# Key tiles of a cross attention moved into three stage boundaries of a fused two-block decoder kernel

## The reference

```python
def reference(x, c, positions, ..., mem_2, ...):
    x = first_block(x, c, positions, ...)
    return second_block(x, mem_2, ...)
```

```python
def cross_attention(h, mem, wq, wkv, wo):
    q = (h @ wq).reshape(B, S, X_HEADS, X_HEAD_DIM)
    k, v = jnp.split(mem @ wkv, 2, axis=-1)
    k = k.reshape(B, M, X_HEADS, X_HEAD_DIM)
    v = v.reshape(B, M, X_HEADS, X_HEAD_DIM)
    s = jnp.einsum("bshd,bmhd->bhsm", q, k).astype(jnp.float32) / math.sqrt(X_HEAD_DIM)
    p = jax.nn.softmax(s, axis=-1).astype(v.dtype)
    o = jnp.einsum("bhsm,bmhd->bshd", p, v).reshape(B, S, X_HEADS * X_HEAD_DIM)
    return o @ wo
```

## Time and profile before

| what | us |
|---|---|
| runs | 1763.84, 1765.99, 1769.26 |
| median | 1765.99 |
| span of the profiled execution, first to last instruction | 1764.7 |
| mean granted TensorE clock | 0.993 of full |
| boundary ahead of feed-forward three | 597.86 to 606.36 |
| boundary ahead of the latent attention | 802.7 to 810.78 |
| boundary ahead of the hybrid mixer | 1140.2 to 1151.51 |
| cross attention, end of the mixer's output product to first value product | 1452.30 to 1479.74 |

### The profile page before, as it was taken

One profiled execution on the slowest core, in us unless ns is written; L12 is line 12 of the kernel. 1 busy time (PEld: TensorE's weight loads), 2 busy tenths in 40 slices (PEclk: granted clock), 3 DMA queues, 4 the chain that ended last, 5 costly groups with the idle time before them and its releaser, 6 DMA issues.

```text
span 1764.7 us, 31956 instructions
## 1 busy us (share of the span) xinstructions
PE 1669.9 (95%) x11230; PEld 1500.6 (85%) x11230; DVE 1290.2 (73%) x2161; ACT 933.4 (53%) x1664; POOL 86.6 (5%) x151
## 2 busy tenths in 40 slices
PE   6899999999999999999999999999988899999998
PEld 5899989888999889998777888898976789988886
DVE  6888888768888888876566666679888565456665
ACT  1544457644444544445575555555467845555553
POOL 2000010300000100000000000000000000000000
PEclk9999999999999999999999999999999999999999
DMA  8888866757888888865433766444633155446561
GB/s 348 311 295 297 306 173 204 156 203 249 300 292 307 236 293 302 294 184 175 131 108 70 240 191 185 148 148 151 186 97 91 49 191 168 143 136 198 191 184 65
DMA packets 123657, 352.76 MB, mean 200 GB/s; under 512 B 9851, under 2 KB 52875, under 8 KB 114225
## 3 DMA queue, kind: packets, MB, share of 16 engines
q1 hardware_dynamic: 108128, 262.18, 46.4%
q10 hardware_dynamic: 12432, 78.65, 13.8%
q0 software_dynamic: 3008, 10.74, 1.9%
HBM read 347.31 MB, written 4.22 MB: 199 GB/s over the span
## 4 chain that ended last, share of the span: by engine, by line
PE 55%; DVE 20%; issue 11%; ACT 8%; DMA 4%; ACTq 1%; POOL 1%; DVEq 0%; POOLq 0%; SPq 0%
PE ps L829 36%; PE ps L1062 8%; PE ps L1063 4%; DVE w_lo L195 4%; DVE arena L358 4%; DVE arena L2680 2%; ACT w_hi L1116 2%; ACT w_hi L189 2%; DVE w_lo L1127 1%; DMA gate_scratch<-gcol 1%; DMA resid<-in_x 1%; DVE resid L1322 1%; DVE act_s L1196 1%; DMA grow<-gate_scratch 1%; ACTq L332 1%
## 5 line engine op out<-in xcount | busy, mean ns | idle before, releaser
L829 PE MATMUL ps<-t_both,w_hi 128*128 128x256 f32 x3952 | 725.9, 285 | 10.1 <-DVE t_both L758 5.7
L829 PEld LDWEIGHTS ps<-t_both,w_hi 128*128 128x128 f32 x3952 | 615.0, 191 | 23.5 <-issue 10.6
L829 PE MATMUL ps<-t_both,w_lo 128*128 128x256 f32 x1976 | 558.5, 283 | 1.3 <-issue 1.3
L195 DVE TENSOR_TENSOR w_lo<-raw,w_hi 128x1024 fp32r<-128x1024 f32 x240 | 288.6, 1222 | 122.6 <-ACT w_hi L189 122.4
L829 PEld LDWEIGHTS ps<-t_both,w_lo 128*128 128x128 f32 x1976 | 376.6, 191 | 0.2
L1127 DVE TENSOR_TENSOR w_lo<-raw,w_hi 128x1024 fp32r<-128x1024 f32 x258 | 313.6, 1221 | 83.0 <-ACT w_hi L1116 82.9
L1116 ACT ACTIVATE w_hi<-raw 128x1024 fp32r<-128x1024 f32 x258 | 268.8, 1053 | 120.2 <-PE ps L829 79.2
L189 ACT ACTIVATE w_hi<-raw 128x1024 fp32r<-128x1024 f32 x240 | 248.2, 1053 | 143.1 <-PE ps L829 99.6
L1062 PE MATMUL ps<-t_both,w_hi 128*128 128x512 f32 x640 | 226.7, 398 | 0.0
L829 PE MATMUL ps<-w_hi,g_hi 128*128 128x512 f32 x440 | 176.8, 402 | 14.4 <-DVE g_lo L1199 11.9
L1063 PE MATMUL ps<-t_both,w_lo 128*128 128x256 f32 x640 | 179.7, 281 | 0.0
(11 more groups left out here) (378 smaller groups left out, 1662.4 us busy)
## 6 DMA issues: line engine op xcount, KB each, us to landing
raw<-in_stream SPq DMA_DIRECT2D x498, 512.0 KB, 4.5
arena<-in_mod_w ACTq DMA_DIRECT2D x72, 1024.0 KB, 7.2
grow<-gate_scratch POOLq DMA_DIRECT2D x6, 512.0 KB, 7.7
u_scratch<-u_keep ACTq DMA_DIRECT2D x1, 3072.0 KB, 36.8
arena<-u_scratch POOLq DMA_DIRECT2D x8, 256.0 KB, 3.3
small<-in_small POOLq DMA_DIRECT2D x1, 1368.0 KB, 11.2
resid<-in_x POOLq DMA_DIRECT2D x1, 1024.0 KB, 18.9
arena<-in_mem POOLq DMA_DIRECT2D x1, 1024.0 KB, 5.4
```

Source lines behind the costliest of these rows:

```text
L195: VE.tensor_tensor(w_lo[:, s, :], raw[:, s, :], w_hi[:, s, :].bitcast(F32), ALU.subtract).then_inc(lo_done, 1)
L829: last = TE.matmul(out, lhs, rhs, start=start and i == 0, stop=stop and i == 2)
```

## The change

The memory is loaded behind the norm of feed-forward two, turned by TensorE in bodies 1 and 2 of that feed-forward (which therefore leave the loop), kept in high parts (ScalarE, which also copies the bank for GpSimd) and low parts (GpSimd) in the arena, stored to DRAM during feed-forward three, loaded back ahead of feed-forward four, and loaded back again in two pieces in the hybrid mixer. Key tiles 0 and 1 are made ahead of the turn of the tokens in the boundary ahead of feed-forward three, 2 and 3 in that ahead of the latent attention, 4 and 5 in that ahead of the hybrid mixer, and 6 there behind the turn. Tile 7 stays in the cross attention. Each boundary's keys are copied from PSUM by ScalarE behind the turn and stored to DRAM; seven are loaded at the end of the hybrid mixer. The stream's order (`ring_order`, `piece_of`) puts the key blocks where they are used. The fillers of the three boundaries go, the banks of the turn are given out anew (the last tiles share a bank with earlier ones and wait until these are emptied), and one block is split within `squares` at the first of the boundaries. The owed low part is paid within `squares` at all three. `x_split(4, ...)` in the cross attention moves from behind the value product to beside its fifth block, and `mod_swap` gets another place.

```diff
@@ squares / turn
+            if splits is not None:
+                pay_lo()
...
+            for _i in range(splits or 0):
+                owed[0] -= 1
+                next_split()
             return diag_at
...
+                diag_at = squares(src, src_ready, late_mod, splits=None if keys is None else keys["splits"])
+                if keys is not None:
+                    for i, to in enumerate(keys["before"]):
+                        key_tile(to, mem_at, keys["ready"])
...
+                    if kt in shares:
+                        if shares[kt] % 2 == 0:
+                            pe.wait_ge(V.sem, emptied[shares[kt]])
+                        else:
+                            pe.wait_ge(A.sem, emptied[shares[kt]])
...
             turned["at"] = (V.n, A.n)
+            if keys is not None:
+                for to in keys["behind"]:
+                    key_tile(to, mem_at, keys["ready"])
+                keys_keep(*keys["keep"])
+                turned["at"] = (V.n, A.n)
             pay_splits()
@@ new functions
+        def mem_turn(pe, g):
+            if g == 0:
+                pe.wait_ge(mem_in, 16)
+            else:
+                pe.wait_ge(mem_kept, 2 * g)
+            for k in (2 * g, 2 * g + 1):
+                for q in range(QT):
+                    last = TE.transpose(ps[6][:, k % 2 * L + q * P:k % 2 * L + (q + 1) * P], mem_raw[:, q, k * P:(k + 1) * P], ident)
+            last.then_inc(mem_turned, 1)
+
+        def mem_hi(act, g):
+            act.wait_ge(mem_turned, g + 1)
+            if g >= 2:
+                act.wait_ge(mem_lowered, g - 1)
+            E.activation(mem_tiles[:, 4 * g:4 * g + 4:2, :], ps[6][:, :].rearrange("p (a b) -> p a b", b=L),
+                         ACT.Copy).then_inc(mem_kept, 1)
+            E.activation(mem_copy[:, g % 2, :], ps[6][:, :], ACT.Copy).then_inc(mem_kept, 1)
+
+        def mem_lo(pool, g):
+            pool.wait_ge(mem_kept, 2 * g + 2)
+            GE.tensor_tensor(mem_tiles[:, 4 * g + 1:4 * g + 4:2, :], mem_copy[:, g % 2, :].rearrange("p (a b) -> p a b", b=L),
+                             mem_tiles[:, 4 * g:4 * g + 4:2, :].bitcast(F32), ALU.subtract).then_inc(mem_lowered, 1)
...
+        def key_tile(to, tiles, ready):
+            h = blocks["pe"]
+            blocks["pe"] += 1
+            s = h % RING
+            @block.tensor
+            def _(pe):
+                pe.wait_ge(lo_done, h + 1)
+                pe.wait_ge(ready[0], ready[1])
+                for k in range(KT):
+                    ws = slice(k * P, (k + 1) * P)
+                    last = triple(to, tiles(k, 0), tiles(k, 1), w_hi[:, s, ws], w_lo[:, s, ws], True, k == 0, k == KT - 1)
+                last.then_inc(used, 1)
+            owed[0] += 1
...
+        def keys_keep(first, n, banks, at):
+            done = blocks["pe"]
+            held = ar(at, n * L)
+            @block.scalar
+            def _(act):
+                act.wait_ge(used, done)
+                for i in range(0, n, 2):
+                    wide = min(2, n - i) * L
+                    E.activation(held[:, i * L:i * L + wide], banks[i // 2][:, 0:wide], ACT.Copy).then_inc(A.sem, A.up())
+            kept = A.n
+            @block.gpsimd
+            def _(pool):
+                pool.wait_ge(A.sem, kept)
+                pool.dma_start(key_dram[:, first * L:(first + n) * L], held).then_inc(keys_stored.sem, keys_stored.up(16))
@@ act_body of ffn
                     if mod is not None and more:
                         mod_load(act, t, mod + 1)
+                    if mems:
+                        mem_hi(act, mems[t])
@@ ffn
+                    if turn_mem:
+                        emit(1, 2, with_mod, (0, 1))
+                        emit(2, 3, with_mod, (2, 3))
+                    emit(3 if turn_mem else 1, FG - 1, with_mod)
...
                     emit(n_mod - 1, n_mod, with_mod)
+                    mem_store()
@@ the three boundaries
-        norm_x(..., late_mod=PRE + 2 * FG, late_load=True, busy=7)
+        norm_x(..., late_mod=PRE + 2 * FG, late_load=True,
+               keys=dict(before=halves(ps[6]), behind=(), ready=(mem_lowered, 4), splits=1,
+                         banks=(4, 5, 0, 1, 2, 7, 3, 0), shares={7: 2}, keep=(0, 2, (ps[6],), 15056)))
...
-        norm_x(..., early=2, busy=7)
+        norm_x(..., early=2,
+               keys=dict(before=halves(ps[6]), behind=(), ready=(mem_lowered, 4), splits=0,
+                         banks=(2, 4, 0, 1, 5, 7, 3, 0), shares={7: 2}, keep=(2, 2, (ps[6],), 15056)))
...
-        norm_x(lambda k, n: col("mix", k, n), early=2, busy=5, after_squares=keep_positions)
+        norm_x(lambda k, n: col("mix", k, n), early=2, after_squares=keep_positions,
+               keys=dict(before=halves(ps[6]), behind=halves(ps[3])[:1], ready=(mem_back, 16), splits=0,
+                         banks=(2, 4, 0, 1, 5, 7, 1, 0), shares={6: 3, 7: 2}, keep=(4, 3, (ps[6], ps[3]), 11504)))
@@ cross attention
-        turn(lambda q: memt[:, q, :], KT)
         add_residual(None)
         out_used = blocks["pe"]
+        acc_free[0], acc_free[1] = (x_ready[0, 1], 0), (x_ready[1, 1], 0)
         x_diag = squares(lambda q: x[:, q, :], dict(x_ready))
-        turned["at"] = (V.n, A.n)
-        columns_product(8, evac_q(kx))
+        pay_splits()
+        key_tile(ps[4][:, 0:L], mem_again, (mem_back, 48))
...
-        rows_product(KT, D, put_off=True)
+        rows_product(KT, D, put_off=True, chained=True, operand=mem_again)
```

More of the change, by code:

```diff
@@ L12 @@
 from contextlib import ExitStack
+import itertools
 import math
@@ L76, with ring_order, piece_of @@
 UP_ORDER = (9, 10, 0, 1, 2, 3, 4, 5, 11, 12, 6, 7, 8)
+THIRD_FFN, LATENT_IN, HYBRID_IN, MEM_KEYS = 169, 235, 331, 400
+AHEAD = {THIRD_FFN: (0, 1), LATENT_IN: (2, 3), HYBRID_IN: (4, 5, 6)}
+def ring_order():
+    early = [MEM_KEYS + t for tiles in AHEAD.values() for t in tiles]
+    order = []
+    for b in range(N_BLOCKS):
+        order += [MEM_KEYS + t for t in AHEAD.get(b, ())]
+        if b not in early:
+            order.append(b)
+    return order
+def piece_of(b):
+    for base in (BY_TILE, BY_TILE + 8, BY_TILE + 16, Z_BY_TILE, LATENT):
+        if base <= b < base + 8:
+            return base, ((b - base) + 6) % 8 if base == LATENT else b - base
+    if AB_OUT <= b < AB_OUT + 12:
+        return None, b + 8 if b < AB_OUT + 4 else b - 4
+    if UP <= b < UP + 13:
+        return None, UP + UP_ORDER[b - UP]
+    return None, b
 def build(nc, a):
@@ L285, in _ @@
+            rounds = n_stream // RING
+            for back, run in itertools.groupby(range(1, rounds), back_of):
+                run = list(run)
+                if back is not None and len(run) > 1:
+                    in_order(run[0], run[-1] + 1, back)
+                else:
+                    for h in range(run[0] * RING, (run[-1] + 1) * RING):
+                        one(h)
+            for h in range(rounds * RING, n_stream):
                 one(h)
@@ L778, in turn @@
                 for k in (kt, kt + 1):
-                    transpose_tile(k, (1,) if by_tokens else (0, 1))
+                    transpose_tile(k, (1,) if by_tokens and k not in shares else (0, 1))
                 empty_tile(kt)
@@ L1325, in _, with halves @@
                         x_ready[q, f] = V.n
+        def halves(bank, n=2):
+            return [bank[:, i * L:(i + 1) * L] for i in range(n)]
         def norm_x(gain, mods=None, ready=None, mods_before=0, early=4, late_mod=None, late_load=False, busy=0,
-                   after_squares=None):
+                   after_squares=None, keys=None):
             if mods is not None:
```

177 lines of the change are left out of this document (118 added, 59 removed).

## The result

Over twenty runs of each kernel the median went from 1765.78 us (1763.67 to 1769.26) to 1768.28 us (1765.22 to 1773.62). The ratio is 1.0014, with a 95% interval from 1.0008 to 1.002: 2.5 us slower (1.4 to 3.5), inside the 0.3% that counts as no change, but on the other side of zero from the forecast of 1764.2 us. The profiled execution of the changed kernel has a span of 1768.5 us; its time was 1770.6 us, 2.1 more, and 2.3 above the median.

What follows compares the result with a forecast made beforehand. TensorE, busy for 95% of the span, was taken as the bound. Terms -24.6 + 2.8 + 3.4 + 5.8 + 10.8 = -1.8 us, from the median 1765.99, gave 1764.2 us; own range 1760.5 to 1768, reaching toward rivals 1755.5 to 1770.

Steps and rivals of the forecast that it cites:

- The reload of 2 MB: Memory reload ahead of the hybrid mixer, in feed-forward four: hidden under a low DMA share, priced at nothing.
- The cross attention: Output product to value product: one key tile stays of 27.44 us, key reload hidden, value product doesn't wait; gain 24.6 us.
- Boundary one: Ahead of feed-forward three: two keys delay the turn 2.5 us, late low parts add 0.9; cost 3.4, bounds 2.5 and 4.9.
- Boundary two: Ahead of the latent attention: five owed low parts delay angles, sines and squares; cost 4.3 plus 1.5 for the clock, 5.8 us.
- the clock, 1.5 us: Behind the 3.4 us wait ahead of boundary two's token sums: TensorE's clock falls, cost 1.5 us, bounds 0 and 3.5.
- Boundary three: Ahead of the hybrid mixer: three keys, 3.4 us wait ahead of the narrow product, clock 1.5; cost 10.8, bounds 5.9 and 12.8.
- Feed-forward two: Memory's work in bodies 1 and 2: ScalarE copies 1.6 us, GpSimd beside VectorE 1.2; cost 2.8, bounds 0.5 and 4.
- GpSimd's contention: Feed-forward two: GpSimd's four low parts stretch VectorE's work by 0.3 us each, 1.2 us; 5.8 if VectorE stood still.
- The first (no waits behind the keys): Rival: VectorE catches up, blocks split in time; boundaries cost 2.5 + 2.2 + 5.9, sum -11.2, 1754.8 us; chance 0.25.
- The second: Rival: clock stays low some 7 us after each of the three boundary gaps; sum +5.7, 1771.7 us; chance 0.09.
- The third: Rival: gate row 6 us late, costing 4, 1768.2 us, chance 0.07; with VectorE stretched by 5.8, 1772.8, chance 0.04.
- the signs that were to show the prediction wrong: Narrow product right behind key 6, feed-forward two growing under 1 or over 5 us, or the value product waiting.

Runs made afterwards that it cites:

- experiment 4: Changed kernel with the 2 MB memory reload issued after the first body of feed-forward four instead of at its entrance; one execution, feed-forward four 186.33 us.
- experiment 1: Changed kernel with the memory reload issued after five bodies of feed-forward four instead of at its entrance; 1763.71 us, ratio 0.9991 to the kernel before.
- experiment 2: Kernel before with an unused 2 MB load added at the entrance of feed-forward four; 1769.72 us, ratio 1.0016 to the kernel before.
- experiment 7: Changed kernel with VectorE's angles at boundary two made behind two of the five low parts, not all five; 1763.84 us, ratio 0.9995 to before.
- experiment 3: Kernel before with an unused 1 MB load added at the entrance of feed-forward four; one execution, feed-forward four 188.04 us.
- Experiment 5: Changed kernel with boundary three's next weight block split inside the norm instead of behind the key copies; 1764.28 us, ratio 0.9984 to before.
- experiment 9: Changed kernel with the memory's four low parts in feed-forward two made by VectorE instead of GpSimd; one execution, feed-forward two 200.34 us.

## Why the prediction was wrong, step by step

**The step that failed** is the sentence "The reload of 2 MB runs under a feed-forward whose DMA share is low", and its price of nothing. It measured 4.16 us. The mean share is indeed no more than 0.64 in that stage before the change, and it was zero just ahead of the issue. But the reload was issued 0.4 us ahead of the ring's first load, at the start of the 24 us in which the DMA engines are taken for over nine tenths. ScalarE waited 8.23 us for a block instead of 2.67, VectorE's and then TensorE's work followed, and behind the 2.25 us gap the clock fell, as it did in all six profiles with the reload at this place and in none without it. Adding the load to the kernel before costs 3 us, taking it away from this place gives 4.7 (the stage is then 0.6 us shorter than before the change, which nothing here explains), and 13 us later it costs nothing; in five further profiles with the reload at the entrance the stage took 191.0 to 193.3 us. So the reload and its place are shown as the cause; what of the entrance's traffic it hinders is open (experiment 4). Without this step the forecast was good: 1764.2 us, against 1763.71 for the kernel of experiment 1.

**The cross attention**, -24.6: -24.63. The value product did not wait; no row shows a price of the key reload.

**Boundary one**, 3.4: 2.60 in the pair of profiles, 3.6 in the means. The 2.60 are made of 2.32 of delay (2.5 forecast) and 0.28 of late low parts (0.9 forecast). TensorE's gap in the first body went from 0.81 to 1.66 us, as forecast. The late low parts cost their 0.9 after all, once profiles with the same clock are compared: feed-forward three without a drop of the clock takes 195.17 us in experiment 2, whose code there is before's, and 196.18 in the changed kernel, 195.96 in experiment 7's.

**Boundary two**, 5.8: 5.25 in the pair, 5.6 in the means. Two steps were right to a tenth of a microsecond: a wait of 3.4 us, released by the squares, measured 3.34; and the clock, 1.5 us, measured 1.59. The start of the first product was delayed by 1.7, not 2.2, in the pair. Before's boundary took 8.51 us there and 8.34 and 7.43 in the kernels of experiments 2 and 3, which have its code, so that against their mean the delay is 2.1. Experiment 7 shows the chain of causes: five low parts, then angles, sines, squares.

**Boundary three**, 10.8: 9.19 + 1.53. Wait of 3.4 us ahead of the narrow product: 3.26. Experiment 5 shows that it hung on the high part behind the key copies. The three keys paid here 10.7 us, and 4.2 more for their reload, to save 8.6 in the cross attention. The gap at this boundary was 2.8 us, room for one:

```profile
1144.08 1.38 PE L425 MATMUL ps<-cst 128*128 128x128 f32 x10
1146.87 3.92 PE L697 MATMUL ps<-arena,resid 128*128 128x128 f32 x32 [1.41 <-ACT arena L578]
```

**Feed-forward two**, 2.8: 1.84. The drop of the clock at 438 is gone, as forecast, but it was not credited. That it is gone says little: in the kernels of experiments 2 and 3 the gap of 2.48 us is still there, and the clock did not fall behind it. Without the drop the stage takes 195.7 us in these two, so the memory's work costs 2.4. GpSimd's contention was put at 1.2 and is some 0.8 by the stretched rows, if body 2 is like body 1.

**The rivals.** The first (no waits behind the keys) is refuted at both places. The second had the clock low for 7 us behind each gap. Behind the narrow product's gap it was 3.4 us each time that it fell, at a price of 1.5; ahead of the token sums it was 3.4 us in three profiles and 6.8 in three, at 1.6 and 2.5; behind boundary one's gap of 1.66 us it never fell. The third had the right kind of cause, transfers, but at the wrong DMA: the store beside feed-forward three landed in 9.2 us, where 11 to 24.5 were thought of. None of the signs that were to show the prediction wrong occurred, as none of them looked at feed-forward four.

**What the single pair of profiles hides.** The rows up to feed-forward two (+1.77) and the mixer (+2.05) differ in this pair by chance, the clock's above all. At the start, eight transposes near 43 us took 1.07 us before and 1.95 in the changed kernel, where the clock was still low; over eleven kernels with the change's code the first product of feed-forward two starts between 401.03 and 404.70, and before's in three profiles between 401.33 and 403.28. In the mixer it was low for 10.2 us in the changed kernel (below). Without those two rows the stages of the pair add to -0.06 us, while the medians say +2.5: before's own profile is slow from feed-forward two to feed-forward four, 551.6 us where experiments 2 and 3, with its code there, took 549.5 and 549.4. The means over all profiles, given with the stages above, close most of that gap; they are rough, with three profiles of before's code.

## What to carry to other kernels

A low DMA share, be it the mean of a stage or the share at the moment of issue, doesn't make a transfer free: ask which transfers are issued just behind it, and when their data is needed. Here 2 MB ahead of the ring's refill cost 4 us or more, and the same 2 MB 13 us later cost nothing, although the DMA engines were then full. Work is worth moving only into a gap that is there: two keys at boundary one cost 3.6 us and save 5.8, three at boundary three cost more than they save until the wait behind them was taken out. Where an entrance has one order of instructions on each engine, adding up that order predicted the two waits within 0.2 us (3.34 and 3.26, both put at 3.4), and putting one split earlier or three low parts later took them away; the first cost nothing that the stages show, the second 1.0 us.

## What the runs showed of the hardware that was not expected

**The clock behind a gap is not the same each time.** In body 1 of feed-forward three all fourteen profiles have the same gap of 2.44 to 2.50 us; behind it the granted clock fell to 1.2 GHz in eleven and stayed at 2.4 GHz in three, the changed kernel's among them. Behind the 3.3 us ahead of the token sums it fell in six of eight. Behind 2.44 to 2.48 us in body 1 of feed-forward two, in the three profiles with before's code, it fell in one; behind 1.91 us in experiment 9's kernel it fell too. Windows of the changed kernel behind the wait of the token sums and in body 1 of feed-forward three, then of experiment 1's kernel behind the wait of the token sums (the last three numbers are the granted clock, the DMA share and GB/s):

```profile
834.00:838.00 4.00, 4.00 (x24) 4.00 (x25) 1.98 (x3) 0.67 (x1) 0.72 (x1) 0.62 0.87 246
...
648.00:652.00 4.00, 3.59 (x19) 3.10 (x20) 3.37 (x5) 2.40 (x3) 0.00 (x0) 1.00 0.84 306
```

```profile
833.50:837.50 4.00, 4.00 (x35) 4.00 (x36) 2.06 (x3) 0.75 (x1) 0.72 (x1) 1.00 0.83 250
```

The same gap of the same work thus gave both outcomes. The Trainium skill, "TensorE: Matmul & The Clock Gate", section "What's actually happening", has the chip judge TensorE's activity in windows that run freely and don't start anew with a kernel. These profiles agree with that and don't prove it.

**What a drop costs depends on the stage.** The drops lasted 3.4 to 10.2 us. One of 3.4 us cost 1.5 where TensorE alone sets the pace (12.09 against 10.56 us behind boundary three; 130.5 against 128.95 behind the token sums), and some 0.6 in the feed-forwards with modulation, where VectorE sets it (196.6 against 196.1, and 196.3 against 195.7 before).

**A drop can come with no gap behind which to put it.** In four of the fourteen profiles the clock was low for 10.2 us in the mixer, 3 us behind a wait of some 0.42 us that is there in all fourteen. One of the four is experiment 3's, whose mixer is that of the kernel before; its way from the 48 wide products to feed-forward five took 2.1 us more. In six other profiles it fell for 3.4 us within 25 us of that place, in four not at all. The windows of that kernel, and of the kernel before:

```profile
1280.00:1290.00 10.00, 10.00 (x64) 9.74 (x64) 4.06 (x9) 1.63 (x3) 0.00 (x0) 0.52 0.21 63
```

```profile
1278.00:1288.00 10.00, 8.62 (x92) 8.23 (x90) 4.89 (x11) 2.81 (x3) 0.00 (x0) 1.00 0.34 100
```

So read the granted clock of both before you believe a difference of 2 us in one stage between two single profiles.
